# Two PSUM banks for the transposes of the joint attention stage, and all transposes of a step ahead of all its value products

## The chip, the cores and the metric

The kernel runs on one core of one Trainium2 chip. The metric is the device time of one execution in microseconds (us). The core's engines work in parallel and meet only at semaphores: PE (TensorE, matrix products and transposes), DVE (VectorE), ACT (ScalarE), POOL (GpSimd) and SP, which here issues DMAs. Each engine takes its own instructions in the order in which they are written.

## What is computed

The reference is one layer of a hybrid encoder for 1024 prompt tokens and 128 sample tokens. The part that matters here is the prompt's forgetting attention (16 heads of width 64, blocks of 128 queries), which runs side by side with a chunkwise mLSTM and, in the second of two stages, with the expert sums (PEER) of earlier tokens.

```python
def fox_block(qb, cq, q_pos, k, v, ck, k_pos):
    s = jnp.einsum('bqhd,bshd->bhqs', qb.astype(jnp.float32), k) * DH_F ** -0.5
    s = s + jnp.swapaxes(cq, 1, 2)[..., :, None] - jnp.swapaxes(ck, 1, 2)[..., None, :]
    s = jnp.where(k_pos[None, :] <= q_pos[:, None], s, -jnp.inf)
    p = jax.nn.softmax(s, axis=-1)
    return jnp.einsum('bhqs,bshd->bqhd', p, v).astype(qb.dtype)
...
        act = jax.nn.gelu(jnp.einsum('thkd,td->thk', u_tab[idx], xb).astype(jnp.float32), approximate=False)
        return jnp.einsum('thk,thkd->td', (g * act).astype(xb.dtype), v_tab[idx])
```

## The kernel before

`trunk_kernel` runs stages one after another. `stage_attend` runs twice. The first call (query blocks 0 to 2, 48 steps) has attention and mLSTM alone. The second call, the **joint stage**, has query blocks 3 to 7 (80 steps) and also gives DVE, ACT and POOL the expert sums of two token tiles.

**A step** s is one head and one query block: head s // 5 and block 3 + s % 5 in the joint stage. I call s % 5 the *place* of the step. Its scores cover 4 + place blocks of 128 keys, so 4 to 8 blocks. Step s is worked on in two passes of the loop over steps:

- in pass s, PE makes the scores (`pe_scores`, L500 and L502, tile `att_psum_fs`, one buffer in the joint stage), DVE takes the row maximum (`dve_max`, L534, `att_fnmax`), and ACT takes the exponential (`act_exp`, L561, `att_fprob`, two buffers);
- in pass s + 1, PE **turns** (transposes) the probabilities, up to four blocks a round, into the PSUM tile `att_psum_ft` (`pe_turn`, L508), ACT copies them to SBUF (`act_probs`, L569, `att_fprobT`), PE **mixes** them with the values into `att_psum_fy` (`pe_mix`, L522), and DVE scales the result (`dve_y`, L541 and L546, `att_fy`).

Five to eight blocks are two rounds, four are one. So the pass at place 1 has one round (4 blocks), and those at places 2, 3, 4 and 0 have two rounds: 5, 6, 7 and 8 blocks. In the first call every step has one round.

**The tile `att_psum_ft` is one PSUM bank.** It is also used by `pe_head` (L484), which transposes a part of the next head's queries or keys in the passes at places 0 to 3, and is emptied by `act_head` (L554). `use` numbers all uses of the bank; `t_full` counts fillings by PE, and `t_free` counts emptyings by ACT. Every filling waits until the one before it has been emptied.

**The order is written by hand.** In each pass both `pe` and `act` have two *slots*, the mLSTM's pieces for that pass (`ml.pe_slot`, `ml.act_slot`, called memory slots); most second slots are empty on PE. PE's pass is: scores of s, head transposes, slot 0, turn round 0 of s - 1, slot 1, mix round 0, turn round 1, mix round 1. ACT's is: head copy, exponential of s, slot 0, copy of round 0, expert half 0 (`act_host`), slot 1, copy of round 1, expert half 1. DVE's is: maximum of s, slot 0, expert half 0, slot 1, `dve_y` of s - 1, expert half 1.

**The expert work** is cut into units of one group of four experts: four dot products on DVE (L2220, `ex_uv`), one product with the gate (L2224, `ex_wt`) and four additions (L2233, `ex_acc`), with a Gelu on ACT between the dots and the gate product (L2265, `ex_act`). A half pass takes 3 or 4 units of the running list. With nine units a group and 36 units in five passes, the Gelu falls in half 1 of the passes at places 0 and 1 and in half 0 of those at places 3 and 4. Exp and Gelu need different tables on ACT, so there is an ACT_TABLE_LOAD between them. POOL issues the indirect DMAs that fetch the experts' rows (L2163).

Of the kernel before, what the change touches and what calls it, by code (L numbers as in the profile page):

```python
# [21 lines left out]
P = 128  # L22
# [7 lines left out]
H_F, DF = 16, 64  # L30
# [19 lines left out]
class Stage:  # L50
# [5 lines left out]
    def __init__(self, nc, tag):  # L56
        self.nc, self.tag, self.ctx, self.held = nc, tag, ExitStack(), []
# [328 lines left out]
class FoxPrompt:  # L386

    def __init__(self, nc, K, st, z, T, b0, b1):
        self.K, self.T, self.b0, self.b1 = K, T, b0, b1
        NB = self.NB = b1 - b0  # L390
        self.STEPS = H_F * NB
        self.W = b1 * P
        self.SBUFS = 1024 // self.W if self.W <= 512 else 1
        self.zr = z[P:TOK, :].rearrange("(t p) n -> p t n", p=P)
        self.q, self.k, self.v = (st.sb(n, [P, 2, w, P]) for n, w in (("fq", NB), ("fk", b1), ("fv", b1)))
        self.qT, self.kT = st.sb("fqT", [DF + 1, 2, NB * P]), st.sb("fkT", [DF + 1, 2, b1 * P])
        self.prob, self.probT = st.sb("fprob", [P, 2, self.W]), st.sb("fprobT", [P, self.W])
        self.nmax, self.total, self.inv = (st.sb(n, [P, 2]) for n in ("fnmax", "ftotal", "finv"))
        self.y = st.sb("fy", [P, 2, NB, P])
        self.s_ps, self.t_ps, self.y_ps = st.ps("fs", [P, 1024]), st.ps("ft", [P, 512]), st.ps("fy", [P, 512])  # L400
        (self.ones_set, self.t_full, self.t_free, self.scored, self.maxed, self.expd, self.inverted, self.mixed,
         self.y_ready) = st.sems("f_ones_set f_t_full f_t_free f_scored f_maxed f_expd f_inverted f_mixed f_y_ready")
        self.qk_in, self.ck_in, self.v_in, self.y_out = (
            [st.sem(f"f_{n}{s}") for s in range(2)] for n in ("qk_in", "ck_in", "v_in", "y_out"))
        self.groups = [(self.q, self.qT, c, min(4, NB - c), DF ** -0.5) for c in range(0, NB, 4)]
        self.groups += [(self.k, self.kT, c, min(4, b1 - c), 1.0) for c in range(0, b1, 4)]
        assert len(self.groups) <= NB
        order = [("head", 0, g) for g in range(len(self.groups))]
        for s in range(self.STEPS + 1):
            order += [("head", hd, g) for hd, g in self.heads_at(s)]  # L410
            if s >= 1:
                order += [("prob", s - 1, r) for r in range(self.rounds(s - 1))]
        self.use = {key: n for n, key in enumerate(order)}

    def heads_at(self, s):
        hd, g = s // self.NB + 1, s % self.NB
        return [(hd, g)] if hd < H_F and g < len(self.groups) else []
# [57 lines left out]
    def pe_head(self, pe, hd, g):  # L475
        src, _, c0, n, _ = self.groups[g]
        i, e = divmod(hd, 2)
        if g == 0:
            pe.wait_ge(self.qk_in[i % 2], (i // 2 + 1) * 32)
        u = self.use["head", hd, g]  # L480
        if u >= 1:
            pe.wait_ge(self.t_free, u)
        for c in range(n):
            mm = pe.transpose(self.t_ps[0:DF, c * P:(c + 1) * P], src[:, i % 2, c0 + c, e * DF:(e + 1) * DF],  # L484
                              self.K["ident"][:])
        mm.then_inc(self.t_full, 1)

# [15 lines left out]

    def pe_turn(self, pe, s, r):
        pe.wait_ge(self.expd, s + 1)
        pe.wait_ge(self.t_free, self.use["prob", s, r])
        for c in range(4 * r, min(4 * r + 4, self.blocks(s))):
            mm = pe.transpose(self.t_ps[:, (c - 4 * r) * P:(c - 4 * r + 1) * P], self.prob[:, s % 2, c * P:(c + 1) * P],  # L508
                              self.K["ident"][:])
        mm.then_inc(self.t_full, 1)  # L510

# [37 lines left out]
    def act_head(self, act, hd, g):  # L549
        _, dst, c0, n, scale = self.groups[g]  # L550
        act.wait_ge(self.t_full, self.use["head", hd, g] + 1)
        if hd >= 2:
            act.wait_ge(self.scored, (hd - 1) * self.NB)
        act.mul(dst[0:DF, hd % 2, c0 * P:(c0 + n) * P], self.t_ps[0:DF, 0:n * P], scale).then_inc(self.t_free, 1)  # L554

    def act_exp(self, act, s):
        act.wait_ge(self.maxed, s + 1)
# [6 lines left out]
    def act_probs(self, act, s, r):  # L564
        n = min(4, self.blocks(s) - 4 * r)
        act.wait_ge(self.t_full, self.use["prob", s, r] + 1)
        if s >= 1:
            act.wait_ge(self.mixed, s)
        act.copy(self.probT[:, 4 * r * P:(4 * r + n) * P], self.t_ps[:, 0:n * P]).then_inc(self.t_free, 1)  # L569


class MlstmPrompt:
# [40 lines left out]
    def claim(self, pe, n):  # L613
        if n >= self.BANKS:
            self.wait_free(pe, n - self.BANKS)
        return self.bank[n % self.BANKS]
# [278 lines left out]
def stage_attend(nc, K, z, gates, C, m, T, b0, b1, ex=None, tiles=0):  # L895

    with Stage(nc, f"att{b0}") as st:
        fx = FoxPrompt(nc, K, st, z, T, b0, b1)
# [14 lines left out]
        def act_host(act, s, half):  # L913
            if not ex or s >= STEPS:
                return
            for g, unit in share(s, half):
                t, r = divmod(g, ex.PER_TILE)
                if unit == 0 and r == 0:
                    ex.act_tile(act, t)
                if unit == ex.G - 1:  # L920
                    ex.act_group(act, 0, r, t)
# [27 lines left out]
        @block.sync  # L949
        def _(sp):  # L950
            fx.sp_first(sp)
            ml.sp_load(sp, 0)
            if ex:
                ex.load(sp, 0)
            for s in range(STEPS):
                fx.sp_step(sp, s)
                for half in range(2):
                    ml.sp_step(sp, *slot(s, half))
                    sp_host(sp, s, half)
            fx.sp_last(sp)  # L960
            ml.sp_last(sp)
            if ex:
                ex.store(sp, tiles - 1)
                ex.stored_all(sp)

        @block.tensor
        def _(pe):
            for g in range(len(fx.groups)):
                fx.pe_head(pe, 0, g)
            for s in range(STEPS + 1):  # L970
                if s < STEPS:
                    fx.pe_scores(pe, s)
                    for hd, g in fx.heads_at(s):
                        fx.pe_head(pe, hd, g)
                    ml.pe_slot(pe, *slot(s, 0))
                if s >= 1:
                    fx.pe_turn(pe, s - 1, 0)
                if s < STEPS:
                    ml.pe_slot(pe, *slot(s, 1))
                if s >= 1:  # L980
                    fx.pe_mix(pe, s - 1, 0)
                    for r in range(1, fx.rounds(s - 1)):
                        fx.pe_turn(pe, s - 1, r)
                        fx.pe_mix(pe, s - 1, r)

        @block.scalar
        def _(act):
            for g in range(len(fx.groups)):
                fx.act_head(act, 0, g)
            for s in range(STEPS + 1):  # L990
                if s < STEPS:
                    for hd, g in fx.heads_at(s):
                        fx.act_head(act, hd, g)
                    fx.act_exp(act, s)
                    ml.act_slot(act, *slot(s, 0))
                if s >= 1:
                    fx.act_probs(act, s - 1, 0)
                act_host(act, s, 0)
                if s < STEPS:
                    ml.act_slot(act, *slot(s, 1))  # L1000
                if s >= 1:
                    for r in range(1, fx.rounds(s - 1)):
                        fx.act_probs(act, s - 1, r)
                act_host(act, s, 1)

        @block.vector
# [1876 lines left out]
```

## Time and profile before

| | |
|---|---|
| median of 3 runs | 5522.59 us (5518.37 to 5522.79) |
| the profiled execution, device time | 5521.03 us |
| its span, first to last instruction | 5519.3 us |
| joint stage, about 2298 to 3226 us of the span | 928 us |
| its DVE busy | 785.95 us (85%) |
| its PE busy | 696.32 us (75%) |
| its ACT busy | 393.56 us (42%) |
| mean granted TensorE clock in it | 0.63 of full speed |
| first attention call, about 628 to 830 us | 202 us |

The page gives for each engine the busy time and what ended its idle time. A view by waits sums, for each waiting line, how long the engine stood and who released it. The timeline lists instructions by start; the bracket behind a row is the idle time of that engine just before it and who ended it. "x8" on a PE row of L522 means eight records. A float32 product leaves two records, so that is four blocks.

### The profile page before, as it was taken

The numbers are of one execution on the slowest core, as the hardware profiler recorded it, in microseconds if no ns is written. First come the engines' busy times: TensorE is split into PE (matmuls) and PEld (weight loads), VectorE is DVE, ScalarE is ACT, GpSimd is POOL, SyncE is SP. The second block draws the span as 40 slices with busy tenths as digits, with TensorE's granted clock in tenths as the row PEclk, the third lists the DMA queues.
The fourth block names the chain that finished last, engine by engine and source line by source line (L and its number), as shares of the span: only waits on it lengthen the run. The fifth ranks groups of instructions, "written<-read, shape, count | busy, mean of one in ns | idle before, by whom it ended". The sixth has DMA issues, their size and how long they took to land. (4 is left out here: it accounts for less than half of the span.)

```text
span 5519.3 us, 50701 instructions
## 1 busy us (share of the span) xinstructions
PE 4644.8 (84%) x16510; PEld 2835.3 (51%) x16510; DVE 3076.5 (56%) x6238; ACT 1036.7 (19%) x1855; POOL 1212.9 (22%) x1162
## 2 busy tenths in 40 slices
PE   4999677978849999677777769884799999999989
PEld 2555464545635555355555536563555445445434
DVE  1000242314565544488888834578777777777743
ACT  2000241111101111244444421112200000000013
POOL 0000001210003333133333300000144444444410
PEclk9999887989979999766666669997999999999999
DMA  2333226557738888788888777744699999999961
GB/s 90 119 119 106 88 63 204 178 195 284 255 118 344 334 313 304 250 322 302 335 328 323 296 283 281 272 160 168 232 418 419 415 419 413 417 417 414 416 240 59
DMA packets 464532, 1478.27 MB, mean 268 GB/s; under 512 B 38290, under 2 KB 204994, under 8 KB 361442
## 3 DMA queue, kind: packets, MB, share of 16 engines
q0 software_dynamic: 119872, 824.76, 37.5%
q1 hardware_dynamic: 344482, 651.36, 33.0%
q8 instruction: 84, 1.38, 0.1%
q14 instruction: 94, 0.77, 0.0%
HBM read 1370.06 MB, written 115.38 MB: 269 GB/s over the span
## 5 line engine op out<-in xcount | busy, mean ns | idle before, releaser
L2163 POOL DMA_INDIRECT ex_uv<-in_uv,ex_here x768 | 1044.5, 1360 | 1926.2 <-DVE ex_acc L2233 1790.8
L2220 DVE CUSTOM_DVE_ANT_0 ex_uv<-ex_uv,ex_xp 128x1024 f32<-128x1024 f32 x768 | 913.2, 1219 | 302.4 <-DMA ex_uv<-in_uv,ex_here 248.0
L2233 DVE SCALAR_TENSOR_TENSOR ex_acc<-ex_uv,ex_wt,ex_acc 128x1024 f32<-128x1024 f32 x768 | 942.3, 1282 | 9.5 <-DVE ex_wt L2224 1.1
L2502 PE MATMUL exp_psum_dn<-exp_dn_big,exp_dn_gg 128*128 128x512 f32 x1536 | 683.9, 595 | 32.0 <-DVE exp_dn_gg L2424 31.9
L2493 PE MATMUL exp_psum_dn<-exp_dn_xT,exp_dn_big 128*128 128x384 f32 x2048 | 682.8, 487 | 13.5 <-DMA exp_dn_big<-in_ud 13.5
L259 PE MATMUL proj_psum_acc<-proj_w,aT_later 128*128 128x385 f32 x1920 | 627.5, 489 | 74.4 <-DMA proj_w<-in_w_in 67.5
L2493 PEld LDWEIGHTS exp_psum_dn<-exp_dn_xT,exp_dn_big 128*128 128x128 f32 x2048 | 389.8, 190 | 312.9 <-issue 61.3
L259 PEld LDWEIGHTS proj_psum_acc<-proj_w,aT_later 128*128 128x128 f32 x1920 | 365.6, 191 | 335.8 <-issue 72.0
L259 PE MATMUL proj_psum_acc<-proj_w,aT 128*128 128x385 f32 x1536 | 501.0, 488 | 9.1 <-DMA proj_w<-in_w_in 9.1
L2502 PEld LDWEIGHTS exp_psum_dn<-exp_dn_big,exp_dn_gg 128*128 128x128 f32 x1536 | 289.9, 190 | 383.1 <-issue 357.6
L522 PE MATMUL att_psum_fy<-att_fv,att_fprobT 128*128 128x64 f32 x1152 | 237.4, 362 | 230.2 <-ACT att_fprobT L569 229.4
L259 PEld LDWEIGHTS proj_psum_acc<-proj_w,aT 128*128 128x128 f32 x1536 | 292.0, 190 | 217.8 <-issue 12.2
L522 PEld LDWEIGHTS att_psum_fy<-att_fv,att_fprobT 128*128 128x128 f32 x1152 | 206.0, 264 | 285.3 <-ACT att_fprobT L569 284.0
L1829 PE MATMUL rt_psum_b<-rt_w,rt_yT 128*128 128x512 f32 x576 | 267.9, 629 | 51.3 <-ACT rt_yT L1895 42.7
L338 DVE MEMSET gate_one<- 128x1024 f32 x2 | 1.8, 912 | 542.7 <-PEq L66 542.7
L1094 POOL DMA_DIRECT2D scratch_ycat<-smp_sy x128 | 61.5, 489 | 1097.7 <-DVE smp_sy L1187 1097.7
L274 ACT COPY proj_zs<-proj_psum_acc 128x385 f32<-128x385 f32 x216 | 103.4, 481 | 971.5 <-PE proj_psum_acc L259 946.7
L1862 PE MATMUL rt_psum_b<-rt_xT,rt_w 128*128 128x128 f32 x2304 | 263.4, 278 | 7.5 <-ACT rt_xT L1895 7.5
L1862 PEld LDWEIGHTS rt_psum_b<-rt_xT,rt_w 128*128 128x128 f32 x2304 | 261.9, 194 | 9.7 <-issue 9.7
L2450 ACT ACTIVATE exp_dn_gg<-exp_psum_dn 128x384 f32<-128x384 f32 x128 | 62.9, 491 | 1055.2 <-PE exp_psum_dn L2493 1045.5
L2224 DVE TENSOR_TENSOR ex_wt<-ex_act,gate 128x4 f32<-128x4 f32 x192 | 31.2, 163 | 401.5 <-ACT ex_act L2265 401.5
L500 PE MATMUL att_psum_fs<-att_fkT,att_fqT 65*128 65x512 f32 (+3 forms) x384 | 249.9, 781 | 3.5 <-ACT att_fprob L561 2.2
(365 smaller groups left out, 4820.8 us busy)
## 6 DMA issues: line engine op xcount, KB each, us to landing
proj_w<-in_w_in SPq DMA_DIRECT2D x48, 1540.0 KB, 12.7
rt_w<-in_w_q SPq DMA_DIRECT2D x36, 2048.0 KB, 8.2
exp_dn_big<-in_ud SPq DMA_DIRECT2D x128, 512.0 KB
exp_dn_big<-in_vd SPq DMA_DIRECT2D x128, 512.0 KB, 7.9
scratch_z<-proj_zs SPq DMA_DIRECT2D x216, 192.5 KB
rt_w<-in_w_br_m SPq DMA_DIRECT2D x18, 2048.0 KB, 10.9
rt_w<-in_w_br_f SPq DMA_DIRECT2D x18, 2048.0 KB, 11.1
rt_w<-in_w_out SPq DMA_DIRECT2D x18, 2048.0 KB, 8.2
```

Of the source, the lines that this page charges most:

```text
L259: mm = pe.matmul(acc[j % SLOTS][:, 0:CW], aT[:, k, t * P:(t + 1) * P], w[:, u, k, :], start=(k == 0), stop=(k == KD - 1))
L274: act.copy(zs[:, j % SLOTS, :], acc[j % SLOTS][:, 0:CW]).then_inc(read, 1)
L500: pe.matmul(out[:, c:c + w], self.qT[:, hd % 2, b * P:(b + 1) * P], self.kT[:, hd % 2, c:c + w], start=True, stop=(c + w != n))
L522: mm = pe.matmul(self.y_ps[:, 0:DF], self.probT[:, c * P:(c + 1) * P], self.v[:, i % 2, c, e * DF:(e + 1) * DF], start=(c == 0), stop=(c = ...
L1829: mm = pe.matmul(b[:], yT[:, u * KD + k, :], ws[:, k, :], start=(k == 0), stop=(k == KD - 1))
L1862: mm = pe.matmul(b[:, c * P:(c + 1) * P], ws[:, k, c * P:(c + 1) * P], xT[:, k, :], start=(k == 0), stop=(k == KD - 1))
L2163: pool.indirect_dma_start(self.uv[:, slot * self.G + j, :], None, self.uv_tab, bass.IndirectOffsetOnAxis(ap=self.here[:, at, j:j + 1], axi ...
L2220: dve.tensor_tensor_reduce(self.uv[:, slot, 0:D], self.uv[:, slot, 0:D], self.xp[:], 1.0, 0.0, ALU.mult, ALU.add, self.dot[:, p % 2, j:j + ...
L2233: dve.scalar_tensor_tensor(out=self.acc[:, j % 2, :], in0=self.uv[:, slot, D:2 * D], scalar=self.wt[:, p % 2, j:j + 1], in1=self.acc[:, j ...
L2450: act.activation(self.gg[:, c % 4, :], self.banks[3][:, c % 2 * 512:c % 2 * 512 + self.TOKENS], ACT.Gelu).then_inc(self.geluted, 1)
L2493: mm = pe.matmul(self.banks[3][:, at:at + self.TOKENS], self.big[:, q % 4, k * P:(k + 1) * P], self.xT[:, k, :], start=(k == 0), stop=(k = ...
L2502: mm = pe.matmul(self.banks[t][:, n * 512:(n + 1) * 512], self.gg[:, 4 + q % 4, t * P:(t + 1) * P], self.big[:, 4 + q % 4, n * 512:(n + 1) ...
```

## The change

There are two edits, and nothing is computed differently.

1. `att_psum_ft` becomes two banks, `t_bank[0]` and `t_bank[1]`, used in turn by number of use (`turns`). A filling waits only until the filling two before it has been emptied (`claim`). With it all eight PSUM banks are taken.
2. In a pass PE makes all rounds of turns, then slot 1, then all rounds of mixing; ACT copies all rounds right after slot 0, ahead of expert half 0 and slot 1.

```diff
-        self.s_ps, self.t_ps, self.y_ps = st.ps("fs", [P, 1024]), st.ps("ft", [P, 512]), st.ps("fy", [P, 512])
+        self.s_ps, self.y_ps = st.ps("fs", [P, 1024]), st.ps("fy", [P, 512])
+        self.t_bank = [st.ps(f"ft{n}", [P, 512]) for n in range(2)]
...
+    def turns(self, *key):
+        return self.t_bank[self.use[key] % 2]
+
+    def claim(self, pe, *key):
+        if self.use[key] >= 2:
+            pe.wait_ge(self.t_free, self.use[key] - 1)
+        return self.turns(*key)
...
     def pe_turn(self, pe, s, r):
         pe.wait_ge(self.expd, s + 1)
-        pe.wait_ge(self.t_free, self.use["prob", s, r])
+        b = self.claim(pe, "prob", s, r)
...
         @block.tensor
                 if s >= 1:
-                    fx.pe_turn(pe, s - 1, 0)
+                    for r in range(fx.rounds(s - 1)):
+                        fx.pe_turn(pe, s - 1, r)
                 if s < STEPS:
                     ml.pe_slot(pe, *slot(s, 1))
                 if s >= 1:
-                    fx.pe_mix(pe, s - 1, 0)
-                    for r in range(1, fx.rounds(s - 1)):
-                        fx.pe_turn(pe, s - 1, r)
+                    for r in range(fx.rounds(s - 1)):
                         fx.pe_mix(pe, s - 1, r)
...
         @block.scalar
                 if s >= 1:
-                    fx.act_probs(act, s - 1, 0)
+                    for r in range(fx.rounds(s - 1)):
+                        fx.act_probs(act, s - 1, r)
                 act_host(act, s, 0)
                 if s < STEPS:
                     ml.act_slot(act, *slot(s, 1))
-                if s >= 1:
-                    for r in range(1, fx.rounds(s - 1)):
-                        fx.act_probs(act, s - 1, r)
                 act_host(act, s, 1)
```

`pe_head`, `act_head` and `act_probs` take their bank from `claim` or `turns` in the same way. Line numbers of the changed kernel are a few higher.

PE in the joint stage, passes 14 and 15 (places 4 and 0, empty memory slots), from the turns of step 13 to the mixing of step 14. Before:

```order
L508 MATMUL att_psum_ft<-ident,att_fprob 128x128 x4
L522 MATMUL att_psum_fy<-att_fv,att_fprobT 128x64 x4
L508 MATMUL att_psum_ft<-ident,att_fprob 128x128 x3
L522 MATMUL att_psum_fy<-att_fv,att_fprobT 128x64 x3
L500 MATMUL att_psum_fs<-att_fkT,att_fqT 128x512
L502 MATMUL att_psum_fs<-mask,ident 128x128
L484 MATMUL att_psum_ft<-ident,att_fq 64x128 x4
L508 MATMUL att_psum_ft<-ident,att_fprob 128x128 x4
L522 MATMUL att_psum_fy<-att_fv,att_fprobT 128x64 x4
L508 MATMUL att_psum_ft<-ident,att_fprob 128x128 x4
L522 MATMUL att_psum_fy<-att_fv,att_fprobT 128x64 x4
```

The same stretch of PE now:

```order
L515 MATMUL att_psum_ft<-ident,att_fprob 128x128 x7
L529 MATMUL att_psum_fy<-att_fv,att_fprobT 128x64 x7
L507 MATMUL att_psum_fs<-att_fkT,att_fqT 128x512
L509 MATMUL att_psum_fs<-mask,ident 128x128
L491 MATMUL att_psum_ft<-ident,att_fq 64x128 x4
L515 MATMUL att_psum_ft<-ident,att_fprob 128x128 x8
L529 MATMUL att_psum_fy<-att_fv,att_fprobT 128x64 x8
```

The second round of turns moved ahead of the first round of mixing, so turns and mixing stand as one block each.

ACT in the joint stage, passes 13 and 14 (places 3 and 4, where the Gelu falls in half 0). Before:

```order
L561 ACTIVATE att_fprob,att_ftotal<-att_psum_fs,att_fnmax 128x896
L569 COPY att_fprobT<-att_psum_ft 128x512
L2265 ACT_TABLE_LOAD
L2265 ACTIVATE ex_act<-ex_dot 128x4
L569 COPY att_fprobT<-att_psum_ft 128x256
L561 ACT_TABLE_LOAD
L561 ACTIVATE att_fprob,att_ftotal<-att_psum_fs,att_fnmax 128x1024
L569 COPY att_fprobT<-att_psum_ft 128x512
L2265 ACT_TABLE_LOAD
L2265 ACTIVATE ex_act<-ex_dot 128x4
L569 COPY att_fprobT<-att_psum_ft 128x384
```

The same stretch of ACT now:

```order
L568 ACTIVATE att_fprob,att_ftotal<-att_psum_fs,att_fnmax 128x896
L576 COPY att_fprobT<-att_psum_ft 128x512
L576 COPY att_fprobT<-att_psum_ft 128x256
L2269 ACT_TABLE_LOAD
L2269 ACTIVATE ex_act<-ex_dot 128x4
L568 ACT_TABLE_LOAD
L568 ACTIVATE att_fprob,att_ftotal<-att_psum_fs,att_fnmax 128x1024
L576 COPY att_fprobT<-att_psum_ft 128x512
L576 COPY att_fprobT<-att_psum_ft 128x384
L2269 ACT_TABLE_LOAD
L2269 ACTIVATE ex_act<-ex_dot 128x4
```

The copy of round 1 moved from behind the Gelu to ahead of its table load.

## Rows read from the trace of the kernel before

**Rows 1.** Stretches: us, busy by engine (instructions), clock, DMA share, GB/s.
```profile
core 0: us, PE busy (x) PEld busy (x) DVE busy (x) ACT busy (x) POOL busy (x), PEclk, DMA share, GB/s
2298.00:3226.00 928.00, 696.32 (x2565) 502.27 (x2563) 785.95 (x1311) 393.56 (x642) 332.04 (x309) 0.63 0.82 310
```

**Rows 2.** Waits of DVE in the joint stage: total us, times, longest.
```profile
DVE ex_wt L2224 <- ACT ex_act L2265: 57.7, 64, 4.2
DVE att_fy L546 <- PE att_psum_fy L522: 31.7, 17, 3.8
DVE att_fy L546 <- issue: 23.3, 10, 3.4
...
DVE att_fy L546 <- DVE att_finv L541: 3.4, 6, 0.9
```

**Rows 3.** Timeline of DVE, passes 14 and 15.
```profile
2473.20 0.28 DVE L546 TENSOR_SCALAR att_fy<-att_psum_fy,att_finv 128x64 f32<-128x64 f32 x1 [2.66 <-PE att_psum_fy L522]
...
2485.80 0.28 DVE L546 TENSOR_SCALAR att_fy<-att_psum_fy,att_finv 128x64 f32<-128x64 f32 x1 [3.42 <-PE att_psum_fy L522]
```

**Rows 4.** Timeline of ACT, pass 14.
```profile
2467.74 0.58 ACT L569 COPY att_fprobT<-att_psum_ft 128x512 f32<-128x512 f32 x1
2468.33 1.28 ACT L2265 ACT_TABLE_LOAD   x1
2470.06 0.20 ACT L2265 ACTIVATE ex_act<-ex_dot 128x4 f32<-128x4 f32 x1 [0.45 <-DVE ex_dot L2220]
2471.01 0.48 ACT L569 COPY att_fprobT<-att_psum_ft 128x384 f32<-128x384 f32 x1 [0.74 <-PE att_psum_ft L508]
```

**Rows 5.** Timeline of PE, passes 14 and 15, clock 0.50.
```profile
2468.36 1.97 PE L522 MATMUL att_psum_fy<-att_fv,att_fprobT 128*128 128x64 f32 x8 [2.23 <-ACT att_fprobT L569]
2470.12 0.85 PE L508 MATMUL att_psum_ft<-ident,att_fprob 128*128 128x128 f32 x3
2471.54 1.54 PE L522 MATMUL att_psum_fy<-att_fv,att_fprobT 128*128 128x64 f32 x6 [0.57 <-ACT att_fprobT L569]
...
2480.22 1.97 PE L522 MATMUL att_psum_fy<-att_fv,att_fprobT 128*128 128x64 f32 x8 [2.17 <-ACT att_fprobT L569]
2481.98 1.06 PE L508 MATMUL att_psum_ft<-ident,att_fprob 128*128 128x128 f32 x4
2483.72 1.97 PE L522 MATMUL att_psum_fy<-att_fv,att_fprobT 128*128 128x64 f32 x8 [0.68 <-ACT att_fprobT L569]
```

**Rows 6.** Timeline of PE, the mixing of pass 50 at full clock.
```profile
2882.11 1.10 PE L522 MATMUL att_psum_fy<-att_fv,att_fprobT 128*128 128x64 f32 x8 [1.04 <-ACT att_fprobT L569]
2883.05 0.61 PE L508 MATMUL att_psum_ft<-ident,att_fprob 128*128 128x128 f32 x4
```

**Rows 7.** Timeline: gate products of passes 13 and 68, ACT's copies there.
```profile
2458.86 0.16 DVE L2224 TENSOR_TENSOR ex_wt<-ex_act,gate 128x4 f32<-128x4 f32 x1 [2.02 <-ACT ex_act L2265]
3086.91 0.16 DVE L2224 TENSOR_TENSOR ex_wt<-ex_act,gate 128x4 f32<-128x4 f32 x1 [4.25 <-ACT ex_act L2265]
3084.77 0.59 ACT L569 COPY att_fprobT<-att_psum_ft 128x512 f32<-128x512 f32 x1 [2.02 <-PE att_psum_ft L508]
2459.79 0.37 ACT L569 COPY att_fprobT<-att_psum_ft 128x256 f32<-128x256 f32 x1 [0.96 <-PE att_psum_ft L508]
```

**Rows 8.** Waits of PE in the joint stage.
```profile
PE att_psum_fy L522 <- ACT att_fprobT L569: 194.6, 141, 7.1
PE att_psum_ft L508 <- ACT att_fkT L554: 16.0, 15, 3.0
PE att_psum_ft L508 <- ACT att_fqT L554: 9.4, 8, 5.2
```

**Rows 9.** Waits of PE in the first attention call.
```profile
PE att_psum_ft L508 <- ACT att_fkT L554: 2.0, 3, 0.7
```

**Rows 10.** Two stretches of the joint stage, columns as in rows 1.
```profile
3006.60:3049.30 42.70, 33.51 (x110) 23.95 (x110) 36.42 (x56) 17.27 (x28) 19.49 (x17) 0.50 0.96 379
2683.70:2717.60 33.90, 26.67 (x134) 19.74 (x132) 29.78 (x55) 18.31 (x33) 11.90 (x11) 0.80 0.92 343
```

More of the change, by code:

```diff
@@ L479, in pe_head @@
             pe.wait_ge(self.qk_in[i % 2], (i // 2 + 1) * 32)
-        u = self.use["head", hd, g]
-        if u >= 1:
-            pe.wait_ge(self.t_free, u)
+        b = self.claim(pe, "head", hd, g)
         for c in range(n):
-            mm = pe.transpose(self.t_ps[0:DF, c * P:(c + 1) * P], src[:, i % 2, c0 + c, e * DF:(e + 1) * DF],
+            mm = pe.transpose(b[0:DF, c * P:(c + 1) * P], src[:, i % 2, c0 + c, e * DF:(e + 1) * DF],
                               self.K["ident"][:])
@@ L505, in pe_turn @@
         pe.wait_ge(self.expd, s + 1)
-        pe.wait_ge(self.t_free, self.use["prob", s, r])
+        b = self.claim(pe, "prob", s, r)
         for c in range(4 * r, min(4 * r + 4, self.blocks(s))):
-            mm = pe.transpose(self.t_ps[:, (c - 4 * r) * P:(c - 4 * r + 1) * P], self.prob[:, s % 2, c * P:(c + 1) * P],
+            mm = pe.transpose(b[:, (c - 4 * r) * P:(c - 4 * r + 1) * P], self.prob[:, s % 2, c * P:(c + 1) * P],
                               self.K["ident"][:])
@@ L553, in act_head @@
             act.wait_ge(self.scored, (hd - 1) * self.NB)
-        act.mul(dst[0:DF, hd % 2, c0 * P:(c0 + n) * P], self.t_ps[0:DF, 0:n * P], scale).then_inc(self.t_free, 1)
+        act.mul(dst[0:DF, hd % 2, c0 * P:(c0 + n) * P], self.turns("head", hd, g)[0:DF, 0:n * P], scale).then_inc(self.t_free, 1)
     def act_exp(self, act, s):
@@ L568, in act_probs @@
             act.wait_ge(self.mixed, s)
-        act.copy(self.probT[:, 4 * r * P:(4 * r + n) * P], self.t_ps[:, 0:n * P]).then_inc(self.t_free, 1)
+        act.copy(self.probT[:, 4 * r * P:(4 * r + n) * P], self.turns("prob", s, r)[:, 0:n * P]).then_inc(self.t_free, 1)
 class MlstmPrompt:
```

## The prediction

> **What bounds the kernel now.** Start with the stretches. Only the two attention calls use the changed code, and the joint stage is where steps have two rounds, so the question is what sets its 928 us [rows 1]. DVE is busy for 786 us of it, PE for 696, ACT for 394. DVE is nearest to the bound but isn't full: it stands for 142 us. Next come its waits, because what an engine near the bound waits for is what an edit can give back. Two lines make up most of the 142 [rows 2]: the scaling of the attention rows, `att_fy`, waits 31.7 + 23.3 + 3.4 = 58.4 us in 33 places, and the gate product, `ex_wt`, waits 57.7 us in 64 places. The 23.3 are put down to "issue", but that line waits for nothing but the mixing and its own reciprocal, so they belong to the mixing too. The rest is the stage's start and short links within DVE.
>
> The timeline then shows what stands behind each. In pass 14 DVE is ready for `att_fy` 2.66 us early, in pass 15 3.42 us [rows 3]. PE's side of the same passes reads: mixing of round 0, turns of round 1, a wait for ACT, mixing of round 1 [rows 5]. Between the two mixings lie a turn and a copy in which PE makes no product. So the path that sets the stage's pace in these passes is: maximum on DVE, exponential on ACT, copy 0, mixing 0, turn 1, copy 1, mixing 1, `att_fy` on DVE.
>
> **What the change takes off.** With a second bank turn 1 stands before mixing 0, where PE waits anyway: 2.23 and 2.17 us ahead of mixing 0 in passes 14 and 15, against 0.85 and 1.06 us for turn 1 [rows 5]. Copy 1 then runs beside mixing 0: 0.48 us [rows 4] against 1.97 us. The end of mixing 1 comes earlier by the whole distance from the end of mixing 0 to the start of mixing 1:
>
> - pass 14 (place 4, 7 blocks): 2471.54 - (2468.36 + 1.97) = 1.21 us;
> - pass 15 (place 0, 8 blocks): 2483.72 - (2480.22 + 1.97) = 1.53 us.
>
> At full clock the distance is little smaller, since it holds a fixed copy: turn 1 of four blocks takes 0.61 us for 1.06 [rows 6]. I take 1.1 there. Where ACT does the Gelu or a memory slot with a table of its own ahead of copy 1, the distance is longer, up to 3.1 us, and it all goes, since copy 1 now stands ahead of both.
>
> DVE can't win more than it waits. Going through its 33 waits in the timeline (first at pass 3, last at 3223.9 us) and taking for each the smaller of wait and distance gives 21.4 us for the 14 waits of place 4 and the stage's last pass (30.7 us of wait), 17.5 us for the 13 of place 0 (24.8 us of wait), and 2.6 us for the rest, nearly all of theirs. **Sum: 41.5 us off**, and 17 us of `att_fy` waits stay. The next thing that is late there is mixing itself: about 3.5 to 4 us of it at half clock after copy 0, against the three dot products that DVE has to do meanwhile.
>
> **What it adds.** Copy 1 now stands ahead of the Gelu wherever the Gelu is in half 0: 16 passes at place 3, 16 at place 4.
>
> - *Place 3.* DVE has one dot product before the gate product, and waits 2.02 us for the chain exponential, copy 0, table load, Gelu (pass 13, [rows 7]). ACT is never idle in that chain, so copy 1 lengthens it by its 0.37 us [rows 7]: 16 x 0.38 = 6.1 us. Against it: in nine of these passes PE's turns come late and the wait is longer, at most 4.25 us, where ACT stood 2.02 us for turn 0 [rows 7]; over all 16 that surplus is 10 us. PE's lag shrinks by about 0.57 us (mixing 1 of the pass before ends that much sooner at place 2) and by its wait for the head's copy, which the second bank takes from ahead of turn 0 (25.4 us in the stage, [rows 8]), so I take half of the surplus, 5 us, as gone. Net **1.2 us on**; the bounds are 6.1 on and 4 off.
> - *Place 4.* Three dot products come first, and ACT stood 0.45 us before the Gelu [rows 4]; copy 1's 0.48 us fits into that but for 0.03. In four passes ACT is later by a memory slot and there is no such gap: 4 x 0.4 us, **1.5 on**.
> - *Slot 1 behind both rounds of turns.* On PE it is empty but for the gate sums and one set of key transposes per 16 passes. It costs nothing, hidden under PE's wait for copy 0 (194.6 us in the stage for both mixings, [rows 8]); if that cover were gone, it would be 1 us in 5 passes.
> - *A wait added.* Turn 1 waits for the head's copy where there is one. Queued behind it on PE is all the mixing. ACT has made this copy before the exponential, and copy 1 comes after the exponential, so it is free by then. Nothing, bounded by the 25.4 us of [rows 8] moving from turn 0 to turn 1.
>
> **First attention call.** One round per step: the order doesn't change, only the bank. PE waits there for a head copy ahead of the turns for 2.0 us on the key side [rows 9] and less on the query side. Together with head transposes that no longer alternate with copies at both stages' starts: **2 us off**, between 0 and 5.
>
> **A rule against the rows.** Two stretches of the joint stage have PE busy for the same share, 33.51 of 42.70 us and 26.67 of 33.90 us, yet the granted clock is 0.50 in one and 0.80 in the other [rows 10]. So the busy share of PE doesn't tell which of its two levels it gets, 1.2 or 2.4 GHz, and I can't derive the clock after the change. I keep 0.63. The Trainium skill (TensorE: Matmul & The Clock Gate, Part 4: PE-mode transpose) says that transposes don't count as activity for the clock gate, which speaks against putting up to eight of them in a row. These two rows are in keeping with it but can't prove it. By that rule the time would be that of rival 1.
>
> **Sum.** -41.5 + 1.2 + 1.5 - 2 = -40.8 us. The profiled execution took 5521.0 us, 1.6 us under the median: 5480.2 for it and **5482 us** against the median of 5522.6. A measurement of this kernel can tell about 0.2% (11 us) from no change.
>
> **The rivals.**
>
> 1. *The clock stays at 1.2 GHz through the joint stage.* Then all mixing takes 1.97 us for four blocks where it now takes 1.10 in part [rows 5, 6]. For it: the run of turns is longer. Against it: the gap of more than a microsecond between the mixings goes. DVE's waits for mixing that stay rise from 17 to about 25 us (mixing 1 would end 5.3 us after the maximum at places 4 and 0, set against when DVE is ready in each pass), and PE's lag at place 3 isn't made up (5 us): 13 us less gain, **5495 us**.
> 2. *The gain is taken back on ACT.* If PE reaches turn 0 late at places 3 and 4, as in pass 68, copy 1 has to wait for turn 1 too, and the Gelu with it: up to 0.85 + 0.48 us [rows 4, 5] at 32 places is 42 us, as much as the gain. Against it: ACT stood for turn 0 for a noticeable time in fewer than half of them. **5520 us**, no change.
> 3. *Slower: PE becomes the bound.* It is busy for 696 us at clock 0.63. About a quarter of the stage runs at the high level; that is some 185 us of work, and at half clock it would be 185 x 0.8 = 148 us more (1.97 to 1.10, [rows 5, 6]), 844 us. If PE also keeps standing for copy 0 in each pass (194.6 us by 141, [rows 8], 1.4 us x 80 = 112 us), its stage is 956 us for 928 now: **5551 us**. It decides from the point at which busy time and the wait before mixing 0 together pass 928. Against it: a PE that runs late finds copy 0 done and doesn't wait.
> 4. *More than forecast.* All 58.4 us of the `att_fy` waits go and the late turns with them, because the clock rises with denser products: about 5458 us.
>
> **How the numbers follow.** Forecast 0.70 (5482, its bounds 5472 to 5493), rival 1 0.12, rival 2 0.07, rival 3 0.04, rival 4 0.07. The range of 8 in 10 takes in rival 1 and half of rival 4: 5464 to 5508. Faster 0.89, no change 0.07, slower 0.04.
>
> **What would show it.** In the changed trace: the joint stage at about 888 us, DVE busy for the same 786; on PE one L529 row of x10 to x16 per pass with no turn between; `att_fy` waits of about 17 us in all, `ex_wt` waits of about 60, and the gate product at place 3 waiting about 2.4 us where it had been 2.02; no wait of copy 1 for turns. I would be wrong if `ex_wt` grew by tens of microseconds (rival 2), if PE were busy for well over 800 us (rivals 1 and 3), or if dot products began to wait for the experts' DMAs, which they don't now.

## Result and profile after

The changed kernel takes **5466.0 us** (median of 4 runs, 5461.4 to 5467.7) against 5520.5 us for the kernel before in the same comparison. The ratio is 0.9904, 95% interval 0.9886 to 0.9921. The forecast was 5482 us with a range of 5464 to 5508. So the sign is as forecast and the time lies near the low end of the range: the change brought 54 us where the sum had 41.

Its profiled execution has a span of 5463.8 us, 55.5 less than before. Two lines of the page and the joint stage, from the first maximum to the last `att_fy`:

```profile
span 5463.8 us, 50701 instructions
...
PE 4587.0 (84%) x16510; PEld 2814.9 (52%) x16510; DVE 3076.7 (56%) x6238; ACT 1029.8 (19%) x1855; POOL 1218.3 (22%) x1162
```

```profile
core 0: us, PE busy (x) PEld busy (x) DVE busy (x) ACT busy (x) POOL busy (x), PEclk, DMA share, GB/s
...
2292.90:3165.80 872.90, 641.92 (x2559) 484.41 (x2557) 784.97 (x1311) 387.11 (x641) 334.19 (x309) 0.67 0.86 328
```

The same stretch of the kernel before, between the same two instructions, is 922.7 us long. DVE's work in it is unchanged (785 us, as in [rows 1]), so the 50 us are idle time of DVE that has gone. Its waits there, to be held against [rows 2]:

```profile
DVE ex_wt L2228 <- ACT ex_act L2269: 54.5, 64, 3.1
...
DVE att_fy L553 <- issue: 3.7, 3, 1.4
DVE att_fy L553 <- PE att_psum_fy L529: 3.4, 4, 1.6
DVE att_fy L553 <- DVE att_finv L548: 1.7, 3, 1.0
```

The `att_fy` waits fell from 58.4 us in 33 places to 8.8 in 10, 49.6 us less. The gate product's waits fell by 3.2. The other 5.4 us of the gain lie ahead: 3.4 in the first attention call (from its first maximum to its last `att_fy` 190.7 us for 194.1) and 2.0 between the gates and the first maximum of the joint stage. What is left over adds up to 0.2 us, by chance in part: code that the change doesn't touch took 1.6 us less ahead of the first call, 1.6 less between the two calls and 3.0 more behind them.

Passes 14 and 15, the counterpart of [rows 3 to 5], in the timeline of the changed kernel (start, length, engine, line):

```profile
2451.70 1.22 DVE L541 TENSOR_REDUCE att_fnmax<-att_psum_fs 128x1 f32<-128x1024 f32 x1
...
2454.06 0.96 ACT L576 COPY att_fprobT<-att_psum_ft 128x512 f32<-128x512 f32 x2
...
2454.69 3.25 PE L529 MATMUL att_psum_fy<-att_fv,att_fprobT 128*128 128x64 f32 x14 [3.74 <-ACT att_fprobT L576]
2455.03 1.28 ACT L2269 ACT_TABLE_LOAD   x1
2456.39 0.21 ACT L2269 ACTIVATE ex_act<-ex_dot 128x4 f32<-128x4 f32 x1
2456.63 0.16 DVE L2228 TENSOR_TENSOR ex_wt<-ex_act,gate 128x4 f32<-128x4 f32 x1 [0.27 <-ACT ex_act L2269]
2458.05 0.28 DVE L553 TENSOR_SCALAR att_fy<-att_psum_fy,att_finv 128x64 f32<-128x64 f32 x1 [1.19 <-PE att_psum_fy L529]
...
2465.07 3.67 PE L529 MATMUL att_psum_fy<-att_fv,att_fprobT 128*128 128x64 f32 x16 [2.17 <-ACT att_fprobT L576]
...
2468.85 0.28 DVE L553 TENSOR_SCALAR att_fy<-att_psum_fy,att_finv 128x64 f32<-128x64 f32 x1 [1.61 <-PE att_psum_fy L529]
```

All seven blocks of pass 14 are mixed in one go, 14 records in 3.25 us; before there was a turn and a copy between eight and six. DVE waits 1.19 us in pass 14 and 1.61 in pass 15, where it waited 2.66 and 3.42 [rows 3]. The gate product of pass 14 waits 0.27 us as before, with both copies ahead of the Gelu's table load.

### The profile page after: what moved, and what is told of

Read it like the earlier page. It is cut to its first block and busy times, and to the rows that moved or that the text cites. A ratio compares the mean times of both kernels' runs of the same rounds, so it can differ in the third digit from the quotient of the medians.

```text
span 5463.8 us, 50701 instructions
## 1 busy us (share of the span) xinstructions
PE 4587.0 (84%) x16510; PEld 2814.9 (52%) x16510; DVE 3076.7 (56%) x6238; ACT 1029.8 (19%) x1855; POOL 1218.3 (22%) x1162
## 5 line engine op out<-in xcount | busy, mean ns | idle before, releaser
L529 PE MATMUL att_psum_fy<-att_fv,att_fprobT 128*128 128x64 f32 x1152 | 218.5, 355 | 239.8 <-ACT att_fprobT L576 239.4
L507 PE MATMUL att_psum_fs<-att_fkT,att_fqT 65*128 65x512 f32 (+3 forms) x384 | 238.1, 748 | 3.5 <-ACT att_fprob L568 2.2
```

The source lines that it names most:

```text
L507: pe.matmul(out[:, c:c + w], self.qT[:, hd % 2, b * P:(b + 1) * P], self.kT[:, hd % 2, c:c + w], start=True, stop=(c + w != n))
L529: mm = pe.matmul(self.y_ps[:, 0:DF], self.probT[:, c * P:(c + 1) * P], self.v[:, i % 2, c, e * DF:(e + 1) * DF], start=(c == 0), stop=(c = ...
```

## Experiments

Theory A is the prediction's: DVE sets the pace, and what is paid back is the time that turn 1 and copy 1 spent between the two mixings. Its rivals are that the second bank itself is what pays (B), that the order alone pays (C), and that a higher clock does (E).

| kernel | median us | ratio to before, 95% interval | joint stage us | `att_fy` waits | `ex_wt` waits |
|---|---|---|---|---|---|
| before | 5520.5 | | 922.7 | 58.4 | 57.7 |
| changed | 5466.0 | 0.9904, 0.9886 to 0.9921 | 872.8 | 8.8 | 54.5 |
| bank_only | 5507.2 | 0.9982, 0.9973 to 0.9992 | 919.3 | 57.4 | 53.8 |
| order_one_bank | 5517.5 | 1.0001, 0.9991 to 1.0010 | 922.2 | 25.5 | 87.5 |
| pe_order_only | 5473.2 | 0.9916, 0.9900 to 0.9933 | 888.3 | 28.7 | 50.8 |
| act_order_only | 5569.4 | 1.0091, 1.0074 to 1.0108 | 981.5 | 35.8 | 133.8 |
| before_warm | 5510.1 | 0.9984, 0.9974 to 0.9993 | 908.2 | 48.3 | 53.0 |
| after_warm | 5462.3 | 0.9900, 0.9882 to 0.9918 | 872.7 | 8.3 | 55.0 |
| copy1_late_at_3 | 5456.7 | 0.9889, 0.9872 to 0.9907 | 868.3 | 8.0 | 50.4 |
| changed_again | 5461.3 | 0.9900, 0.9883 to 0.9916 | 873.4 | 9.6 | 54.6 |
| late_at_3_again | 5456.6 | 0.9890, 0.9873 to 0.9906 | 868.4 | 9.0 | 49.8 |

The joint stage is taken from its first maximum to its last `att_fy`. The waits are DVE's in it, from each kernel's own profiled execution. Each ratio is to runs of the kernel before on the same chip: it took 5516.8 us beside the four kernels from bank_only to act_order_only, 5520.6 beside the two warm ones and copy1_late_at_3, and 5517.7 beside the last two.

### The second bank alone

```diff
 # the changed kernel, with the loops over rounds on PE and ACT as before
-                    for r in range(fx.rounds(s - 1)):
-                        fx.pe_turn(pe, s - 1, r)
+                    fx.pe_turn(pe, s - 1, 0)
...
+                    fx.pe_mix(pe, s - 1, 0)
+                    for r in range(1, fx.rounds(s - 1)):
+                        fx.pe_turn(pe, s - 1, r)
+                        fx.pe_mix(pe, s - 1, r)
```

> Two banks, with the order of before on PE and ACT. Theory A (the gain is that turn 1 and copy 1 leave the gap between the two mixings): a second bank alone takes away only PE's waits for a head copy ahead of the turns and ahead of the first head transposes. The waits of att_fy in the joint stage stay at about 58 us, and the time falls by 3 us in the first attention call, 2 at the start of the joint stage and 3 by earlier turns at place 3: 5512 us. Rival B (PE was held by the single bank, so the bank is what pays): att_fy waits fall to under 30 us and the time is below 5490 us.

It took 5507.2 us. The waits of DVE on the attention rows stay as they were:

```profile
DVE ex_wt L2231 <- ACT ex_act L2272: 53.8, 64, 3.7
DVE att_fy L553 <- PE att_psum_fy L529: 31.4, 18, 3.8
DVE att_fy L553 <- issue: 22.9, 10, 3.4
```

So a single bank was not what held up the joint stage: rival B falls. The bank is worth 3.4 us there, all of it in the late Gelus of place 3 (39.2 us of waits for 42.5), as forecast. In the first attention call it came to 6.2 us where I expected 3. The mean clock of the joint stage was 0.65 here for 0.63 before, and the `att_fy` waits stayed.

### The new order with one bank

```diff
     def turns(self, *key):
-        return self.t_bank[self.use[key] % 2]
+        return self.t_bank[0]
     def claim(self, pe, *key):
-        if self.use[key] >= 2:
-            pe.wait_ge(self.t_free, self.use[key] - 1)
+        if self.use[key] >= 1:
+            pe.wait_ge(self.t_free, self.use[key])
```

> The new order on PE and ACT with one bank: turn 1 waits for copy 0, and all mixing comes behind turn 1. Theory A: at half clock mixing ends about 0.6 us sooner than before at places 4 and 0 (only copy 1 has left the path), which is worth some 18 us plus about 5 us in passes with a table in ACT's slot 1; but copy 1 now waits for turn 1 ahead of the Gelu, and the gate product at place 3 waits about 1 us longer than before, 16 us on. 5515 us, with ex_wt waits of 70 to 75 us. Rival C (the order alone is what pays): within 10 us of the changed kernel, 5466 to 5476 us.

It took 5517.5 us, no change from before. PE now stands for copy 0 ahead of turn 1, once in each of the 64 passes with two rounds, and ACT's copy 1 holds up the Gelu:

```profile
PE att_psum_ft L515 <- ACT att_fprobT L576: 186.7, 64, 8.9
```
```profile
DVE ex_wt L2228 <- ACT ex_act L2269: 87.5, 64, 4.5
DVE att_fy L553 <- issue: 13.6, 7, 2.9
```

`att_fy` waits fell by 33 us and `ex_wt` waits rose by 30. I had 23 and 16; both were too small, and the errors cancel. Rival C falls: neither half of the change brings more than 10 us of its own, and together they bring 54. The 186.7 us show what the bank is for: with one bank turn 1 can't be made before copy 0 is done.

### The order of one engine at a time, with two banks

```diff
 # pe_order_only: ACT as before
-                    for r in range(fx.rounds(s - 1)):
-                        fx.act_probs(act, s - 1, r)
+                    fx.act_probs(act, s - 1, 0)
...
+                    for r in range(1, fx.rounds(s - 1)):
+                        fx.act_probs(act, s - 1, r)
```

> Two banks and the new order on PE, the order of before on ACT: copy 1 stands behind the Gelu of half 0 and slot 1 again. Theory A: place 0 has no Gelu in half 0 and keeps all its gain; at place 4 mixing 1 waits for copy 1 and ends 0.7 us later than in the changed kernel, and up to 3 us later in four passes with a table load in slot 1: 13 us on. At place 3 the gate product waits 2.0 us again where it waited 2.3 to 2.4: 6 us off. 5473 us, with att_fy waits near 20 us and ex_wt waits near 49. Rival D (copy 1 ahead of the Gelu costs more than it gives): below 5460 us.

It took 5473.2 us, the time expected, but by waits that were not: `att_fy` 28.7 us for an expected 20 and `ex_wt` 50.8 for 49, with the joint stage 15.5 us longer than the changed kernel's. Rival D falls. In pass 14 the Gelu now stands between the copies again, and mixing is in two pieces:

```profile
2455.78 1.97 PE L529 MATMUL att_psum_fy<-att_fv,att_fprobT 128*128 128x64 f32 x8 [2.68 <-ACT att_fprobT L576]
2457.47 0.21 ACT L2271 ACTIVATE ex_act<-ex_dot 128x4 f32<-128x4 f32 x1 [0.45 <-DVE ex_dot L2226]
2457.59 0.46 ACT L576 COPY att_fprobT<-att_psum_ft 128x384 f32<-128x384 f32 x1
...
2458.10 1.54 PE L529 MATMUL att_psum_fy<-att_fv,att_fprobT 128*128 128x64 f32 x6 [0.35 <-ACT att_fprobT L576]
...
2459.75 0.28 DVE L553 TENSOR_SCALAR att_fy<-att_psum_fy,att_finv 128x64 f32<-128x64 f32 x1 [1.80 <-PE att_psum_fy L529]
```

With two banks, most of the gain is PE's order. ACT's order is the rest: it costs 3.1 us at place 3 (`ex_wt` waits there 35.9 against 39.0) and gives back 14.5 us of `att_fy` waits at place 4 (19.0 against 4.5) and 4.6 at place 0. The edit in reverse, ACT's new order on PE's old one, is the price of rival 2 in full:

> Two banks and the new order on ACT, the order of before on PE: turn 1 comes behind mixing 0, and copy 1, with the Gelu behind it, waits for it. Theory A: this is the price of rival 2 of the prediction in full. The Gelu comes about 2.8 us later at place 3 (45 us on in all); at place 4 it comes 2.7 us later, which mostly takes the place of the att_fy wait (8 us on); the bank gives its 8 us. About 5565 us, ex_wt waits over 130 us. If ex_wt waits stay near 60 us, the chain exponential, copies, table load, Gelu isn't what the gate product waits for.

It took 5569.4 us, 0.9% slower than before. In pass 13 copy 1 waits 2.48 us for a turn that comes behind mixing 0, and everything behind it on ACT waits too:

```profile
2453.10 1.97 PE L529 MATMUL att_psum_fy<-att_fv,att_fprobT 128*128 128x64 f32 x8 [1.69 <-ACT att_fprobT L576]
...
2455.53 0.37 ACT L576 COPY att_fprobT<-att_psum_ft 128x256 f32<-128x256 f32 x1 [2.48 <-PE att_psum_ft L515]
2455.92 1.28 ACT L2270 ACT_TABLE_LOAD   x1
...
2457.21 0.21 ACT L2270 ACTIVATE ex_act<-ex_dot 128x4 f32<-128x4 f32 x1
2457.45 0.16 DVE L2229 TENSOR_TENSOR ex_wt<-ex_act,gate 128x4 f32<-128x4 f32 x1 [4.87 <-ACT ex_act L2270]
```

The gate product there waits 4.87 us for 2.02 [rows 7], 2.85 us more for an expected 2.8. Over the stage the parts were less well sized: at place 3 the waits rose by 33 us (75.9 for 42.5) where I had 45, and at place 4 `ex_wt` rose by 43 and took the place of 29 us of `att_fy`, 14 net where I had 8. This shows that the chain exponential, copies, table load, Gelu is what the gate product waits for. It also shows what keeps rival 2 away in the changed kernel: turn 1 is already there when copy 1 comes.

### How much is the clock

```diff
     def pe_mix(self, pe, s, r):
         n = self.blocks(s)
+        if r == 0 and s >= 1:
+            pe.wait_ge(self.y_ready, s)
+            if self.b0 > 0:
+                for _ in range(3):
+                    pe.matmul(self.y_ps[:, 3 * P:4 * P], self.K["ident"][:], self.K["ident"][:], start=True, stop=True)
         pe.wait_ge(self.t_free, self.use["prob", s, r] + 1)
```

> The kernel before with three extra 128x128 products per pass of the joint stage, put where PE waits for copy 0, into spare columns of the bank of att_psum_fy; they are added work and their result isn't read. They ask how much of the att_fy waits is the clock. Theory E (mixing at half clock is a large part of the 58 us): the granted clock of the joint stage rises from 0.63 to over 0.85, mixing 0 and 1 take 1.1 instead of 2.0 us, att_fy waits fall to about 20 to 30 us and the time to about 5490 us. Rival F (the clock doesn't follow such products, or they make PE late): clock under 0.70 and the time within 10 us of before or above it.

> The changed kernel with the same three extra products per pass. If the clock rises as in the kernel before, the 8.8 us of att_fy waits that stay fall to under 3 us and the turns that are still late at place 3 come earlier (2 us): about 5458 us, so the change is worth about 30 us at a high clock against 54 at the present one. If the products make PE late, the gate products wait longer and the time is above 5466 us.

The first took 5510.1 us, the second 5462.3 (the changed kernel itself took 5466.0 and 5461.3 in two comparisons). In both the wait for `y_ready` also stands ahead of the wait for copy 0, in the first attention call too; no wait is left out. The added products moved the mean clock of the joint stage much less than I thought:

```profile
2292.00:3211.00 919.00, 694.51 (x3050) 528.11 (x3050) 785.43 (x1311) 394.06 (x645) 331.70 (x309) 0.71 0.84 314
```
```profile
2292.00:3164.00 872.00, 658.27 (x3032) 519.78 (x3030) 784.13 (x1309) 386.78 (x641) 334.29 (x309) 0.74 0.87 328
```

The first row is the kernel before with the added products (clock 0.71 for 0.63), the second the changed kernel with them (0.74 for 0.67). Both expectations of the clock were wrong (over 0.85), and with them the 5490 us of theory E; rival F, with a clock under 0.70 and a time within 10 us, was close but isn't met to the letter either. What the pair does show is the size of the term: with the added products 10 us of `att_fy` waits went from the kernel before (48.3 for 58.4) and next to none from the changed one (8.3 for 8.8, where I expected under 3). That it is the clock can be read pass by pass: where the mixing ran at the same clock in before and before_warm, the waits are 0.9 us longer in all; where the clock differs, mostly upward, they are 10.9 us shorter. So a higher clock had 10 us to give in the kernel before and hardly anything in the changed one. What the change would be worth at full clock stays open.

### A better version

At place 3 DVE waits for the Gelu, and `att_fy` has room: the changed kernel has no `att_fy` wait there. So copy 1 can go behind the Gelu there and nowhere else:

```diff
+                late = s >= 1 and s < STEPS and ex is not None and s % fx.NB == 3
                 if s >= 1:
-                    for r in range(fx.rounds(s - 1)):
+                    for r in range(1 if late else fx.rounds(s - 1)):
                         fx.act_probs(act, s - 1, r)
                 act_host(act, s, 0)
+                if late:
+                    for r in range(1, fx.rounds(s - 1)):
+                        fx.act_probs(act, s - 1, r)
```

> The changed kernel with copy 1 behind the Gelu again, but only in the 16 passes at place 3 of the joint stage. Theory A: there DVE waits for the Gelu (2.3 to 2.4 us) and isn't waiting for mixing, so copy 1's 0.37 us comes off the gate product's wait 16 times and nothing is late for it: ex_wt waits 48 to 49 us for 54.5, att_fy waits unchanged, 6 us less than the changed kernel. Rival G (mixing at place 3 becomes late and DVE waits for it instead): ex_wt falls as said, att_fy waits rise by about as much, no difference.

> The changed kernel itself, beside the next one on the same chip. Both theories: 5466 us within 5, the joint stage within 3 us of 873 us, att_fy waits under 12 us.

> The kernel with copy 1 behind the Gelu at place 3 alone, a second time, now beside the changed kernel on the same chip. Its first run was 9 us under the changed kernel, of which its joint stage explains 4.5. Theory A: 4 to 6 us under the changed kernel, all of it in the joint stage (868 to 869 us). If the 9 us were this edit's, the joint stage would have to be near 864 us.

It took 5456.7 and 5456.6 us in two comparisons, the changed kernel beside the second one 5461.3 (4 runs each, 5452.3 to 5459.3 against 5458.8 to 5466.1). Waits of DVE in the joint stage, first of the changed kernel's second run, then of this one beside it:

```profile
DVE ex_wt L2228 <- ACT ex_act L2269: 54.6, 64, 3.1
```
```profile
DVE ex_wt L2232 <- ACT ex_act L2273: 49.8, 64, 2.7
...
DVE att_fy L553 <- issue: 3.9, 3, 1.5
DVE att_fy L553 <- PE att_psum_fy L529: 3.1, 5, 1.2
```

4.8 us of Gelu waits have gone (4.1 in the first pair), a little less than the 6 us expected, and none came back as `att_fy` waits, so rival G falls. The joint stage is 5.0 us shorter (868.4 for 873.4). The two medians differ by 4.6 us, with run ranges that overlap slightly; the stage's length, equal within 0.2 us in both traces of this kernel and within 0.6 in both of the changed one, is the firmer evidence. Of the 9.0 us between the profiled executions of the first pair, 4.5 lie in the joint stage and 4.3 in unchanged code behind it, so about half was chance.

## Why the prediction was right, and where it was short

- **DVE sets the pace, and `att_fy` waits for the second mixing.** Right. DVE's busy time stayed at 785 us and the joint stage shrank by 49.9 us, by 49.6 us of `att_fy` waits and 3.2 of `ex_wt` waits, less 1.9 us more idle time ahead of dot products and about 1 us in waits too short for the view. One of those dot products waited 0.4 us for an expert's DMA, the sign that the prediction named; it stayed at that one.
- **The cut is the distance between the mixings, and DVE wins no more than it waits.** Right in mechanism, undersized: 41.5 us forecast, 49.6 measured. Two things were missed. First, joining two mixings also removes the tail of the first. Four blocks take 1.97 us and three take 1.54 [rows 5], 3.51 together, but seven in one run take 3.25; eight take 3.67 for 3.94. Adding 0.26 us to each distance and counting the same waits again gives 46.5 us. (The ends of products are modelled in this profile; in the five passes where mixing ran at clock 0.50 in both kernels and DVE still waits clearly, 14, 15, 29, 64 and 79, the old wait less distance less 0.26 us gives the new wait within 0.02 us.) Second, some 3 us remain, and the traces show the clock behind them. In passes 19, 30, 45, 49, 70 and 75 the waits fell by 3.2 us more than distance and tail explain, and in all six the mixing ran at a higher clock than before; in pass 5 it ran at 0.50 for 0.76, and 0.4 us of wait stayed that should have gone. Pass 45 is the clearest: 16 records at 0.50 before, at 0.79 now, in 2.44 us where pass 15 takes 3.67. DVE's wait before and now:

```profile
2832.06 0.28 DVE L546 TENSOR_SCALAR att_fy<-att_psum_fy,att_finv 128x64 f32<-128x64 f32 x1 [3.40 <-issue]
```
```profile
2794.41 2.44 PE L529 MATMUL att_psum_fy<-att_fv,att_fprobT 128*128 128x64 f32 x16 [2.17 <-ACT att_fprobT L576]
...
2796.95 0.28 DVE L553 TENSOR_SCALAR att_fy<-att_psum_fy,att_finv 128x64 f32<-128x64 f32 x1 [0.37 <-DVE att_finv L548]
```

  Why the clock was higher in these passes stays open: the stage's mean was 0.67 in this execution and 0.66 in changed_again, 0.63 before. The prediction kept 0.63.
- **Copy 1 ahead of the Gelu at place 3, 0.38 us each, less 5 us for turns that come sooner.** The signs of both terms were right, that of their sum wasn't. The wait rises to 2.29 us in pass 13 where it was 2.02 [rows 7], 0.27 and not 0.38: two copies in a row overlap by 0.1 us (0.85 us for both in the row below, for 0.58 and 0.37). And of the 10 us of surplus I took half as gone; 7.8 went. Net 3.5 us less (39.0 for 42.5) instead of 1.2 more.

```profile
2442.78 0.85 ACT L576 COPY att_fprobT<-att_psum_ft 128x512 f32<-128x512 f32 x2
...
2445.18 0.16 DVE L2228 TENSOR_TENSOR ex_wt<-ex_act,gate 128x4 f32<-128x4 f32 x1 [2.29 <-ACT ex_act L2269]
```

- **Place 4, 1.5 us on.** Measured 0.3 on. The four waits named went to 0.86 us each, three of them from 0.48, as forecast; the wait of pass 4 fell from 1.21 to 0.31 us because ACT no longer waits there for a late turn, which the sum didn't have.
- **First call and start of the joint stage, 2 us off.** Measured 5.4 us, just past the bound of 5. The start gave 2.0. PE's waits for a head copy ahead of the turns, the 2.0 us of [rows 9] and 1.3 on the query side, are gone. That part is right; its size isn't settled closer than a few microseconds, since the call's length moves from one execution to the next: see the last section.
- **Turn 1's new wait for the head's copy is free.** Right: PE waits ahead of the turns for 2.8 us in the changed joint stage, where it waited 25.4 [rows 8], and ACT's copies wait for turns for 4.4 us in all.

```profile
PE att_psum_ft L515 <- ACT att_fkT L561: 2.8, 2, 1.4
```
```profile
ACT att_fprobT L576 <- PE att_psum_ft L515: 4.4, 7, 2.2
```

- **Rival 1 (clock low through the stage).** It didn't happen: 0.67 for 0.63 with up to eight turns in a row. The clock was at 0.50 for whole passes in both kernels, 24 of 80 before and 15 of 80 now. No run here varies the turns alone, so whether they count for the clock stays open.
- **Rival 2 (gain taken back on ACT).** Real as a mechanism, and absent here: `act_order_only` and `order_one_bank` show its price, 76 and 30 us of `ex_wt` waits.
- **Rival 3 (PE becomes the bound).** It didn't happen: PE's busy time fell to 642 us. Two of its steps don't hold in the trace before. Its 112 us for the wait ahead of mixing 0 took the mean over both mixings; ahead of mixing 0 alone PE stood about 150 us. And a late PE doesn't find copy 0 done, it only waits less: in passes 23, 28 and 68, where ACT waited for turn 0, PE still stood 0.68 us for the copy.
- **Rival 4 (more than forecast).** The result lies between the forecast and this, which named the two terms that were short: nearly all `att_fy` waits and the late turns.

## What to carry to other kernels

When a chain alternates between two engines (turn, copy, mix, turn, copy, mix), take the waits of the engine that sets the pace and cut each by the whole distance between the two pieces of work, but by no more than the wait itself; then add the pipeline tail that joining them saves. A second buffer and a new order can be worth 0.2% and nothing alone, and a percent together. Before a short operation is moved ahead of another on an in-order engine, look in each kind of pass at who waits for what stands behind it: the same copy is worth having early at place 4 and late at place 3.

## What the runs showed that I had not expected

- Float32 products of 64 columns into one accumulator: eight records take 1.97 us and sixteen 3.67 at half clock, 0.27 us less than twice the time of eight.
- Two ACT copies in a row of 512 and 256 columns take 0.85 us, for 0.58 and 0.37 apart.
- The first attention call has the same instructions in all kernels with two banks, yet its length ran from 187.9 to 190.7 us over their eight executions, mostly the shorter the higher the granted clock. Which of the two follows the other isn't shown. The rows are the kernel with the bank alone and the changed kernel, first maximum to last `att_fy`:

```profile
629.80:817.80 188.00, 149.46 (x854) 121.31 (x852) 81.17 (x285) 82.13 (x226) 0.00 (x0) 0.90 0.22 67
```
```profile
630.90:821.70 190.80, 152.24 (x854) 123.48 (x852) 81.37 (x285) 82.28 (x226) 0.00 (x0) 0.88 0.22 67
```

  The kernels with one bank fit in: 194.1 us at clock 0.87 before, 193.9 at 0.87 in order_one_bank, and 199.4 us at 0.84 in before_warm, which has no added products in this call. So no execution with one bank was as short as the longest with two, but a difference of 3 us between two single executions of this call says nothing.
- Three added 128x128 products in every pass of the joint stage raised its mean clock by only 0.07 to 0.08. The clock still stood at 0.50 for 19 of 80 whole passes in before_warm, and for 6 in after_warm.
